# The first block's mixers: input and output projections as three one-pass products of split operands

## The chip, the cores and the metric

The kernel runs on one core of a Trainium2 chip. The core has TensorE (matrix products), VectorE, ScalarE and GpSimd (elementwise work, on their own instruction queues) and SyncE, whose queue issues the weight DMAs. The profile calls them PE (and PEld for weight loads), DVE, ACT, POOL and SP. The metric is the device time of one execution in microseconds.

## The reference

Two transformer blocks of two layers each, D = 1024, 256 tokens, all in fp32. The change is in the mixer of the first block; one of its layers, cut:

```python
h = h + 0.5 * swiglu(rmsnorm(h, ffn1_norm[i]), ...)                  # ffn1
u = rmsnorm(h, mix_norm[i]) @ w_in[i]                                # input projections
c_q, c_kv, k_rope, m_x, m_v, m_o, m_if, f_in = split_cols(u, IN_SPLITS)
y_mla = mla_mixer(c_q, c_kv, k_rope, ...)                            # attention, 4 heads
y_mlstm = mlstm_mixer(m_x, m_v, m_o, m_if, ...)                      # conv, gates, two scans
y_fnet = fnet_mixer(f_in, fnet_w[i], fnet_b[i])                      # DFT as products
h = h + jnp.concatenate([y_mla, y_mlstm, y_fnet], axis=-1) @ w_out[i]  # out projection
h = h + 0.5 * swiglu(rmsnorm(h, ffn2_norm[i]), ...)                  # ffn2
```

`w_in` is 1024 x 1744, `w_out` 1024 x 1024. Then follows a gated embedding (`ple`), and after both layers the second block.

## The kernel before

Activations lie feature-major: eight tiles of 128 features by 256 tokens. Weights come as chunks of 128 x 2048 fp32 (1 MB) in a fixed order through a ring of four slots; SyncE loads the next chunk into a slot when that slot's `used` semaphore says so. All engines run one hand-ordered program each, stage after stage (`ffn1`, `mix1`, `ffn2`, `ple` per layer), with waits on semaphores; PSUM is two groups of four banks, `low` and `high`, used in turn.

In the FFNs the products are of split operands: ScalarE copies a chunk to a rounded type that TensorE multiplies in one pass (`split_high`, line 774, into `w_split`), VectorE subtracts that from the chunk (`split_low`, line 811), the same is done with the activations (`x_split`, `a_split`), and `mm3` adds high x high, high x low and low x high. A split chunk frees its ring slot at once; two split buffers alternate, and ScalarE waits on `split_used` for TensorE. Each FFN has 33 chunks, the last 11 of them for the down product (48 one-pass products of 256 columns a chunk).

In the mixer stage `mix1` the products are plain fp32, straight from the ring. `mix1_tensor` first takes `first_projection` (chunk 0, eight k steps of two products, each k as soon as ScalarE has written `xn` for it, line 1190), then the sum of the squares, which GpSimd has added up (line 1221), then chunk 1, the gates (chunk 2, also the conv products), chunk 3 (the m_v values), chunks 4 and 5, the latent sums, chunks 6 and 7 with gate rows between. Each of these chunks but the gates' has 16 products of 128 x 128 by 256 columns. Attention, mLSTM and Fourier mixing follow, and `out_projection` (four chunks, 64 products; source `sq`). VectorE evicts and scales most of it (line 2104), ScalarE the rest; in `mix1_vector`, `head_out` (lines 2162 to 2167) makes the mLSTM output, `transposed_probs` (line 2189) copies a head's transposed softmax for TensorE's value product, and after the out projection each of eight tiles is added to h (line 2310), followed by the low part of the next FFN's x (`plain_low_parts`, line 1205); ScalarE makes the high part (line 1187) and the squares (line 1194). Both also do the next FFN's first two chunk splits between these tiles, after tiles 4 to 6.

At the end of `ffn1` VectorE adds each of the eight down tiles to h (line 1170) and ScalarE follows with `xn` and the square. In layer 0 the rotary table is made just ahead of this (`setup_vector`, lines 4628 to 4650, then `setup_scalar`, lines 4659 to 4661).

Of the kernel before, what the change touches and what calls it, by code (L numbers as in the profile page):

```python
# [25 lines left out]
P = 128  # L26
# [368 lines left out]
def split_count(kind):  # L395
# [33 lines left out]
    "ada_part",  # L429
    "square_in", "square_sum", "plain_root", "gate_part", "gate_scaled", "gate_act", "up_part", "up_scaled", "act_ready", "scale_cols", "rinv_done",  # L430
# [124 lines left out]
class Shared:  # L555


    def __init__(self, nc, ctx, args):
# [6 lines left out]
        self.ring = sb("ring", [P, SLOTS, CHUNK])  # L565
# [19 lines left out]
        with ExitStack() as halves:  # L585
# [7 lines left out]
            self.half_ring = sb_halves("half_ring", [P, 2, 2, KT, P], F32R)  # L593

# [778 lines left out]
def plain_ffn_scalar(act, l, kind):  # L1373
# [91 lines left out]
    if kind == "ffn1":  # L1465
        plain_prepare_scalar(act, g.vec(f"mix_norm{l}"), ready, split=False)
# [14 lines left out]
def plain_ffn_vector(dve, l, kind):  # L1481
# [107 lines left out]
    dve.skip("high", FT)  # L1589
    for j in range(KT):  # L1590
        side = "low" if j < 4 else "high"
        dve.wait_ge(g.sem[side + "_full"], dve.tiles[side] + 1)
        residual_add(dve, j, dve.tile(side), side, 0.5, g.first_x if kind == "ffn1" and l == 0 else None)


def mix1_buffers(g):
# [42 lines left out]

def mix1_tensor(pe, l, kind):  # L1640
# [3 lines left out]
    xn = g.xn  # L1644
# [21 lines left out]
    def feature_pair():  # L1666
        w = weights(KT, 256)
        feature_tile(w, 0)
        feature_tile(w, 1)
        pe.release()  # L1670
        return pe.tiles["low"]

# [54 lines left out]
    first_projection(pe)  # L1727
    plain_sum_tensor(pe)
    feature_pair()
# [21 lines left out]
    w = weights(KT, 256)  # L1751
    for t in range(2):
        tile = low_tile()
        for k in range(KT):
            pe.mm(tile[:, 0:256], xn[:, k, t * P:(t + 1) * P], w[:, k, :], k == 0, k == KT - 1,
                  full="low" if k == KT - 1 else None)
    pe.release()
# [10 lines left out]
    feature_pair()  # L1768
    rope_tile = feature_pair()
# [3 lines left out]
    w = weights(KT, 256)  # L1773
# [9 lines left out]
    pe.release()  # L1783
# [7 lines left out]
    w = weights(KT, 256)  # L1791
# [3 lines left out]
    pe.release()  # L1795
# [125 lines left out]
def mix1_scalar(act, l, kind):  # L1921
# [2906 lines left out]
```

## Time and profile before

| | us |
|---|---|
| median of 3 runs | 3188.19 (3186.05 to 3196.56) |
| the profiled execution | 3193.88 (span 3192.1) |
| TensorE busy | 3150.0, 99% |
| VectorE, ScalarE, GpSimd busy | 1949.2, 1276.8, 97.3 |
| mean granted TensorE clock | 0.997 |
| mix1, layer 0 | 203.0 to 353.8 |
| mix1, layer 1 | 774.8 to 925.4 |

A timeline row gives the start in us, the duration, the engine, the line, the operation with the tiles it writes and reads, its shape and how many instructions are merged in it; in brackets stands the idle time before it and who ended it. A plain fp32 product has two records, so x32 are 16 products; a one-pass product has one. Nearly all matmuls go through one helper (line 526), so tiles tell them apart.

### The profile page before, as it was taken

How to read it: one execution, taken by the hardware profiler on the slowest of the kernel's cores; microseconds unless marked ns; L12 is line 12 of the kernel's file. 1: busy time of each engine (PE TensorE's matmuls, PEld its weight loads, DVE VectorE, ACT ScalarE, POOL GpSimd, SP SyncE). 2: the span in 40 equal slices, each digit the busy share in tenths (PEclk: the TensorE clock that was granted, in tenths of full speed). 3: DMA queues.
4: the chain of work that ended last, by engine and by line, in shares of the span. 5: the costliest groups of instructions: out<-in, count | busy, mean ns of one | idle time of the engine just before them, and what ended most of it. 6: DMA issues, size and time to landing. Idle time of an engine off the chain costs nothing.

```text
span 3192.1 us, 53025 instructions
## 1 busy us (share of the span) xinstructions
PE 3150.0 (99%) x21274; PEld 2685.9 (84%) x21274; DVE 1949.2 (61%) x2974; ACT 1276.8 (40%) x1999; POOL 97.3 (3%) x106
## 2 busy tenths in 40 slices
PE   9999999999999999999999999999999999999999
PEld 8997889889778988888788888878887888876899
DVE  6755574774457556767776677557744676346444
ACT  5444454553345462222544344442224222244433
POOL 0000000000010010000000000000000000000000
PEclk9999999999999999999999999999999999999999
DMA  7543454454345435545222000035532444221353
GB/s 270 184 146 142 175 185 171 178 186 157 139 172 179 176 119 190 185 171 191 93 80 80 3 3 3 28 127 190 205 124 79 171 186 183 97 74 40 134 183 131
DMA packets 62489, 441.25 MB, mean 138 GB/s; under 512 B 6769, under 2 KB 8945, under 8 KB 9329
## 3 DMA queue, kind: packets, MB, share of 16 engines
q1 hardware_dynamic: 60992, 437.39, 37.6%
q8 instruction: 126, 2.06, 0.3%
q10 hardware_dynamic: 1328, 1.46, 0.1%
q14 instruction: 43, 0.34, 0.0%
HBM read 437.77 MB, written 1.05 MB: 137 GB/s over the span
## 4 chain that ended last, share of the span: by engine, by line
PE 91%; DVE 4%; ACT 3%; issue 1%; DMA 0%; POOL 0%; DVEq 0%; ACTq 0%; SPq 0%; POOLq 0%
PE ps_high L526 47%; PE ps_low L526 43%; PE ps_high L535 1%; ACT sb_w_split L774 1%; DVE sb_w_split L811 0%; DVE sb_arena L2151 0%; PE ps_low L535 0%; DVE sb_x_split L2908 0%; ACT sb_arena L2816 0%; DVE sb_silu L2926 0%; ACT sb_xn L2807 0%; DMA sb_ring<-weights 0%; DVE sb_arena L2114 0%; DVE sb_rinv L4495 0%; ACT sb_arena L1972 0%
## 5 line engine op out<-in xcount | busy, mean ns | idle before, releaser
L774 ACT ACTIVATE sb_w_split<-sb_ring 128x2048 fp32r<-128x2048 f32 x260 | 498.6, 1918 | 890.6 <-PE ps_low L526 697.5
L811 DVE TENSOR_TENSOR sb_w_split<-sb_ring,sb_w_split 128x2048 fp32r<-128x2048 f32 x260 | 597.6, 2298 | 257.1 <-ACT sb_w_split L774 257.1
L526 PE MATMUL ps_low<-sb_x_split,sb_w_split 128*128 128x512 f32 (+1 forms) x3520 | 691.2, 354 | 8.3 <-DVE sb_w_split L811 4.0
L526 PE MATMUL ps_high<-sb_x_split,sb_w_split 128*128 128x512 f32 (+1 forms) x3520 | 686.9, 353 | 0.3 <-DVE sb_w_split L811 0.3
L526 PEld LDWEIGHTS ps_low<-sb_x_split,sb_w_split 128*128 128x128 f32 x3520 | 579.0, 189 | 108.0 <-DVE sb_x_split L2908 6.0
L526 PEld LDWEIGHTS ps_high<-sb_x_split,sb_w_split 128*128 128x128 f32 x3520 | 580.3, 189 | 94.7 <-DVE sb_w_split L811 0.6
L526 PE MATMUL ps_low<-sb_a_split,sb_w_split 128*128 128x256 f32 (+1 forms) x2112 | 370.2, 325 | 0.0
L526 PE MATMUL ps_high<-sb_a_split,sb_w_split 128*128 128x256 f32 (+1 forms) x2112 | 365.7, 323 | 0.0
L526 PEld LDWEIGHTS ps_low<-sb_a_split,sb_w_split 128*128 128x128 f32 x2112 | 314.2, 190 | 37.6 <-DVE sb_w_split L811 2.6
L526 PEld LDWEIGHTS ps_high<-sb_a_split,sb_w_split 128*128 128x128 f32 x2112 | 314.9, 190 | 30.9
L1024 DVE SCALAR_TENSOR_TENSOR sb_rest<-sb_ring,sb_consts 128x1024 f32<-128x1024 f32 x256 | 313.3, 1224 | 27.1 <-DVE sb_rest L1024 7.7
L526 PE MATMUL ps_low<-sb_xn,sb_ring 128*128 128x256 f32 (+1 forms) x800 | 183.7, 388 | 0.5 <-ACT sb_xn L2840 0.5
L526 PEld LDWEIGHTS ps_low<-sb_xn,sb_ring 128*128 128x128 f32 x800 | 151.3, 190 | 29.9 <-issue 10.2
L526 PE MATMUL ps_high<-sb_x_split,sb_half_ring 128*128 128x512 f32 x720 | 171.5, 394 | 0.0
L1109 DVE TENSOR_TENSOR sb_a_split<-sb_arena,sb_a_split 128x1024 fp32r<-128x1024 f32 (+1 forms) x44 | 48.0, 1091 | 193.9 <-ACT sb_a_split L1057 193.9
L526 PEld LDWEIGHTS ps_high<-sb_x_split,sb_half_ring 128*128 128x128 f32 x720 | 133.0, 188 | 26.8
L1102 DVE TENSOR_TENSOR sb_arena<-sb_silu,ps_high 128x512 f32 (+3 forms) x88 | 54.5, 620 | 88.8 <-PE ps_high L526 88.8
L1532 DVE TENSOR_TENSOR sb_a_split<-sb_arena,sb_a_split 128x512 fp32r<-128x512 f32 x44 | 30.4, 691 | 111.7 <-ACT sb_a_split L1402 111.7
L1049 ACT ACTIVATE sb_silu<-ps_low 128x512 f32<-128x512 f32 (+1 forms) x88 | 46.9, 533 | 111.4 <-PE ps_low L526 111.4
L2757 POOL TENSOR_TENSOR sb_arena<-sb_arena 128x512 f32<-128x512 f32 (+1 forms) x27 | 33.7, 1250 | 1795.6 <-ACT sb_arena L2816 1793.9
L526 PE MATMUL ps_high<-sb_sq,sb_ring 128*128 128x256 f32 x384 | 83.6, 380 | 1.6 <-issue 1.6
L526 PEld LDWEIGHTS ps_high<-sb_sq,sb_ring 128*128 128x128 f32 x384 | 72.7, 190 | 12.6 <-issue 2.9
(404 smaller groups left out, 3221.0 us busy)
## 6 DMA issues: line engine op xcount, KB each, us to landing
sb_ring<-weights SPq DMA_DIRECT2D x412, 1024.0 KB, 4.8
sb_consts<-consts SPq DMA_DIRECT2D x1, 2148.0 KB, 18.3
sb_sq<-xT SPq DMA_DIRECT2D x1, 1024.0 KB, 5.6
sb_ring<-weights SPq DMA_DIRECT2D x2, 512.0 KB, 7.5
sb_h<-ctxT ACTq DMA_DIRECT2D x1, 1024.0 KB, 15.5
out<-sb_h SPq DMA_DIRECT2D x1, 512.0 KB, 3.0
sb_vectors<-vectors ACTq DMA_DIRECT2D x1, 269.0 KB, 5.8
out<-sb_h SPq DMA_DIRECT2D x1, 256.0 KB, 2.6
```

The source lines that it names most:

```text
L526: ins = self.g.nc.tensor.matmul(out, lhsT, rhs, start=start, stop=stop)
L535: ins = self.g.nc.tensor.transpose(out, in_, self.g.const("identity")[0:n, 0:n])
L774: g.nc.scalar.activation(g.w_split[:, 0, s % 2, :], g.ring[:, n % SLOTS, :], ACT.Copy).then_inc(g.sem["w_high"], 1)
L811: g.nc.vector.tensor_tensor(g.w_split[:, 1, s % 2, :], g.ring[:, n % SLOTS, :], g.w_split[:, 0, s % 2, :].bitcast(F32), ALU.subtract).then ...
L1024: ins = g.nc.vector.scalar_tensor_tensor(scratch, tiles[:, op // STREAMS, :], 1.0, rows[:, op % STREAMS, :], ALU.mult, ALU.mult, accum_out ...
L1049: nc.scalar.activation(g.silu[:, f % 2, 0:width], g.banks["low"][(low + f) % 4][:, 0:width], ACT.Silu).then_inc(g.sem["low_free"], 1)
L1102: nc.vector.tensor_tensor(out, g.silu[:, f % 2, 0:width], g.banks["high"][(high + f) % 4][:, 0:width], ALU.mult).then_inc(g.sem["high_free ...
L1109: nc.vector.tensor_tensor(g.a_split[:, 1, c % 2, :, 0:width], act_in[:, bass.ds(at, 2), 0:width], g.a_split[:, 0, c % 2, :, 0:width].bitca ...
L1532: v.tensor_tensor(g.a_split[:, 1, c % 2, :, 0:TOK], act_in[:, bass.ds(at, 2), 0:TOK], g.a_split[:, 0, c % 2, :, 0:TOK].bitcast(F32), ALU.s ...
L2757: g.nc.gpsimd.tensor_tensor(squares[:, 0, 0:width], squares[:, k, 0:width], squares[:, 0, 0:width], ALU.add).then_inc(g.sem["norm_sum"], p ...
```

## The change

The seven large input chunks (`MIXER_INPUTS`, all but the gates') and the four output chunks are split too. ScalarE writes a chunk's high part (`mixer_split_scalar`) into a half of `w_split` or into `gates_high`, a new buffer over part of the arena; VectorE writes the low part over the chunk in its ring slot (`ring_low`), so the slot is free only when TensorE is done with it, as before. TensorE does `mm3` with both. x is split by `plain_prepare_scalar(..., split=True)` and `plain_low_parts` at the end of `ffn1`; `xn` is no longer made. The gates stay in fp32 and take the high and the low part of x one after the other. The mixed outputs are split as well: ScalarE writes the high part and VectorE subtracts, for the four heads both straight from PSUM, where before ScalarE alone copied the value product into `sq`. The arena's buffers get another order. The core of the diff:

```diff
@@ plain_ffn_scalar, behind after_down @@
     if kind == "ffn1":
-        plain_prepare_scalar(act, g.vec(f"mix_norm{l}"), ready, split=False)
+        for m in (1, 0):
+            mixer_split_scalar(act, l, m, act.chunks + FFN_CHUNKS, act.splits + FFN_CHUNKS)
+        plain_prepare_scalar(act, g.vec(f"mix_norm{l}"), ready, split=True)
@@ plain_ffn_vector, behind setup_vector @@
+    if kind == "ffn1":
+        for m in (1, 0):
+            mixer_split_vector(dve, m, dve.chunks + FFN_CHUNKS, dve.splits + FFN_CHUNKS)
     for j in range(KT):
...
         residual_add(dve, j, dve.tile(side), side, 0.5, g.first_x if kind == "ffn1" and l == 0 else None)
+        if kind == "ffn1" and j:
+            plain_low_parts(dve, g.vec(f"mix_norm{l}"), j - 1, "mix1", l)
+    if kind == "ffn1":
+        plain_low_parts(dve, g.vec(f"mix_norm{l}"), KT - 1, "mix1", l)
@@ new @@
+def mixer_split_scalar(act, l, m, first, splits):
+    g = act.g
+    n = first + MIXER_CHUNKS[m]
+    act.wait_ge(g.landed[n % SLOTS], 16 * (n // SLOTS + 1))
+    if m == 0:
+        act.wait_ge(g.sem["split_used"], splits - 1)
+    elif m == 1:
+        act.wait_ge(g.used[(first - 1) % SLOTS], (first - 1) // SLOTS + 1)
+    elif m == 2:
+        act.wait_ge(g.sem["split_used"], splits)
+    else:
+        act.wait_ge(g.sem["mixer_used"], MIXER_SPLITS * l + m - 1)
+    g.nc.scalar.activation(mixer_high(g, splits, m), g.ring[:, n % SLOTS, :],
+                           ACT.Copy).then_inc(g.sem["mixer_high"], act.adds("mixer_high"))
+
+def mixer_split_vector(dve, m, first, splits):
+    g = dve.g
+    n = first + MIXER_CHUNKS[m]
+    dve.wait_ge(g.sem["mixer_high"], dve.due("mixer_high"))
+    g.nc.vector.tensor_tensor(g.ring_low[:, n % SLOTS, :], g.ring[:, n % SLOTS, :],
+                              mixer_high(g, splits, m).bitcast(F32),
+                              ALU.subtract).then_inc(g.sem["mixer_low"], dve.adds("mixer_low"))
@@ mix1_tensor: feature_tile, likewise the m_v product; first_projection becomes first_pair @@
-            pe.mm(tile[:, 0:TOK], w[:, k, m * P:(m + 1) * P], xn[:, k, 0:TOK], k == 0, k == KT - 1,
-                  full="low" if k == KT - 1 else None)
+            mm3(pe, tile[:, 0:TOK], [part[:, k, m * P:(m + 1) * P] for part in w], mixer_x(g, k), k == 0, k == KT - 1,
+                full="low" if k == KT - 1 else None)
@@ the gates @@
+            for n, x in enumerate(mixer_x(g, k, slice(t * P, (t + 1) * P))):
+                last = k == KT - 1 and n == 1
+                pe.mm(tile[:, t * GATE_SPREAD:(t + 1) * GATE_SPREAD], x.bitcast(F32),
...
@@ mix1_tensor, end @@
-    pe.wait_ge(g.sem["mix_done"], pe.due("mix_done", 2))
+    pe.wait_ge(g.sem["mixed_low"], pe.due("mixed_low", 4))
     pe.wait_ge(g.sem["low_free"], pe.tiles["low"])
-    out_projection(pe, TOK)
+    mixer_out_projection(pe)
@@ mix1_scalar: chunks 2 to 6 behind the root, the second Silu, the m_v evictions and each set of squares; then @@
     root(LH)
+    for k in (6, 7):
+        mixed_high(act, k, g.sq[:, k, 0:TOK])
+    for p in range(2):
+        act.wait_ge(g.sem["mix_done"], act.due("mix_done"))
+        mixed_high(act, 4 + p, g.sq[:, 4 + p, 0:TOK])
+        mixer_split_scalar(act, l, len(MIXER_INPUTS) + p, act.chunks, act.splits)
     ada_units_scalar(act, 0, rows, 1)
...
-        evict(g.sq[:, h, 0:TOK])
+        act.wait_ge(g.sem["low_full"], act.tiles["low"] + 1)
+        mixed_high(act, h, act.tile("low", peek=True)[:, 0:TOK])
+        act.other_frees("low")
@@ mix1_vector: 2 and 3 behind the level memset, 4 behind gate_abs, 5 ahead of latents[4], 6 behind k_rope; then @@
     head_out(1)
+    for k in (6, 7, 4):
+        mixed_low_of(k)
+    mixer_split_vector(dve, len(MIXER_INPUTS), dve.chunks, dve.splits)
+    mixed_low_of(5)
+    mixer_split_vector(dve, len(MIXER_INPUTS) + 1, dve.chunks, dve.splits)
     transposed_probs(1)
+    ada_units_vector(dve, 1)
     transposed_probs(2)
+    head_low(0)
+    ada_sum_vector(dve)
     transposed_probs(3)
-    ada_units_vector(dve, 1)
-    for h in range(H):
-        if h == 1:
-            ada_sum_vector(dve)
-        dve.skip("low")
+    for h in range(1, H):
+        head_low(h)
@@ the loop over the eight out tiles, ScalarE and VectorE alike @@
+        if j in (1, 3):
+            mixer_split_vector(dve, len(MIXER_INPUTS) + 2 + j // 2, dve.chunks, dve.splits)
```

The numbers m in the split functions count the split chunks: m = 0 and 1 are chunks 0 and 1 of the stage, m = 2 to 6 are chunks 3 to 7, m = 7 to 10 the four output chunks.

## Rows read from the trace of the kernel before

**Rows 1.** The page: busy time of each engine, and the chain by engine.
```profile
PE 3150.0 (99%) x21274; PEld 2685.9 (84%) x21274; DVE 1949.2 (61%) x2974; ACT 1276.8 (40%) x1999; POOL 97.3 (3%) x106
PE 91%; DVE 4%; ACT 3%; issue 1%; DMA 0%; POOL 0%; DVEq 0%; ACTq 0%; SPq 0%; POOLq 0%
```
**Rows 2.** Timeline of TensorE, 203 to 222 us: start, us, engine, line, operation, count.
```profile
203.04 7.07 PE L526 MATMUL ps_low<-sb_xn,sb_ring 128*128 128x256 f32 x32
...
210.37 7.07 PE L526 MATMUL ps_low<-sb_xn,sb_ring 128*128 128x256 f32 x32
217.28 0.38 PE L535 MATMUL ps_high<-sb_consts,sb_rinv 128*128 128x128 f32 x2
217.50 3.68 PE L526 MATMUL ps_low<-sb_ring,sb_xn 128*128 128x64 f32 x32
221.02 1.95 PE L526 MATMUL ps_high<-sb_arena,sb_ring 128*128 128x256 f32 x8
```
**Rows 3.** Timeline at the end of the first FFN of each layer.
```profile
201.99 0.49 ACT L1190 ACTIVATE sb_xn<-sb_h,sb_vectors 128x256 f32<-128x256 f32 x1
...
766.64 2.28 DVE L811 TENSOR_TENSOR sb_w_split<-sb_ring,sb_w_split 128x2048 fp32r<-128x2048 f32 x1
...
774.84 7.07 PE L526 MATMUL ps_low<-sb_xn,sb_ring 128*128 128x256 f32 x32
```
**Rows 4.** Timeline of TensorE, out projection and the FFN behind it, layer 0.
```profile
326.25 27.86 PE L526 MATMUL ps_high<-sb_sq,sb_ring 128*128 128x256 f32 x128 [0.52 <-issue]
353.76 5.91 PE L526 MATMUL ps_low<-sb_x_split,sb_w_split 128*128 128x512 f32 x32
359.50 5.80 PE L526 MATMUL ps_high<-sb_x_split,sb_w_split 128*128 128x512 f32 x32
```
**Rows 5.** Timeline of TensorE in a down product, layer 0.
```profile
137.91 1.59 PE L526 MATMUL ps_low<-sb_a_split,sb_w_split 128*128 128x256 f32 x12
...
143.66 1.60 PE L526 MATMUL ps_low<-sb_a_split,sb_w_split 128*128 128x256 f32 x12
```
**Rows 6.** Timeline at the end of attention, layer 0.
```profile
319.67 0.42 DVE L2167 TENSOR_TENSOR sb_sq<-sb_sq,sb_arena 128x256 f32<-128x256 f32 x1
320.01 1.28 DVE L2189 COPY sb_arena<-ps_high 128x512 f32<-128x512 f32 x2
320.75 1.13 PE L526 MATMUL ps_low<-sb_arena 128*128 128x256 f32 x4 [2.55 <-DVE sb_arena L2189]
```
**Rows 7.** Groups by line: the two halves of a weight chunk's split.
```profile
L774 ACT ACTIVATE sb_w_split<-sb_ring 128x2048 fp32r<-128x2048 f32 x260 | 498.6, 1918 | 890.6 <-PE ps_low L526 697.5
L811 DVE TENSOR_TENSOR sb_w_split<-sb_ring,sb_w_split 128x2048 fp32r<-128x2048 f32 x260 | 597.6, 2298 | 257.1 <-ACT sb_w_split L774 257.1
```
**Rows 8.** Timeline beside the out projection: VectorE, GpSimd and ScalarE.
```profile
345.14 0.73 POOL L1221 TENSOR_TENSOR sb_root<-sb_rest,sb_root 128x256 f32<-128x256 f32 x1 [2.73 <-ACT sb_rest L1194]
...
347.98 2.28 DVE L811 TENSOR_TENSOR sb_w_split<-sb_ring,sb_w_split 128x2048 fp32r<-128x2048 f32 x1
348.59 2.25 POOL L1221 TENSOR_TENSOR sb_root<-sb_rest,sb_root 128x256 f32<-128x256 f32 x1 [2.73 <-ACT sb_rest L1194]
...
350.69 0.42 DVE L2310 TENSOR_TENSOR sb_h<-ps_high,sb_h 128x256 f32<-128x256 f32 x1 [0.43 <-PE ps_high L526]
351.04 0.47 DVE L1205 SCALAR_TENSOR_TENSOR sb_x_split<-sb_h,sb_vectors,sb_x_split 128x256 fp32r<-128x256 f32 x1
351.15 0.51 ACT L1187 ACTIVATE sb_x_split<-sb_h,sb_vectors 128x256 fp32r<-128x256 f32 x1 [2.64 <-DVE sb_h L2310]
```
**Rows 9.** Timeline in the middle of the projections, layer 0.
```profile
241.14 0.42 DVE L2104 TENSOR_TENSOR sb_arena<-ps_low,sb_rinv 128x256 f32<-128x256 f32 x1
...
244.40 2.32 PE L526 MATMUL ps_high<-sb_sq,sb_consts 128*128 128x256 f32 x10
```
**Rows 10.** Busy time by stretch; the third number from the end is the granted clock.
```profile
322.00:323.00 1.00, 1.00 (x5) 0.91 (x4) 0.43 (x1) 0.30 (x1) 0.00 (x0) 0.50 0.30 123
...
324.00:325.00 1.00, 1.00 (x4) 0.79 (x3) 0.00 (x0) 0.38 (x1) 0.00 (x0) 0.50 0.00 0
```

More of the change, by code:

```diff
@@ new lines, in mixer_split_vector, with mixer_weights @@
+def mixer_split_vector(dve, m, first, splits):
[5 more added lines that the diff above has]
+                              ALU.subtract).then_inc(g.sem["mixer_low"], dve.adds("mixer_low"))
+def mixer_weights(pe, m):
+    g = pe.g
+    pe.wait_ge(g.sem["mixer_low"], pe.due("mixer_low"))
+    low = g.ring_low[:, pe.chunks % SLOTS, :]
+    pe.chunks += 1
+    return [part.rearrange("p (k n) -> p k n", k=KT) for part in (mixer_high(g, pe.splits, m), low)]
@@ new lines, in mixer_release, with mixer_x, mixed_parts, mixed_high @@
+def mixer_release(pe):
+    pe.release()
+    pe.unreleased.append(pe.g.sem["mixer_used"])
+def mixer_x(g, k, cols=slice(0, TOK)):
+    return [g.x_split[:, 0, k, half][:, cols] for half in (RIGHT, LEFT)]
+def mixed_parts(g, k):
+    return [g.x_split[:, 1, k, half] for half in (RIGHT, LEFT)]
+def mixed_high(act, k, source):
+    g = act.g
+    g.nc.scalar.activation(mixed_parts(g, k)[0], source, ACT.Copy).then_inc(g.sem["mixed_high"], act.adds("mixed_high"))
+def mixed_low(dve, k, source):
+    g = dve.g
+    dve.wait_ge(g.sem["mixed_high"], dve.due("mixed_high"))
+    high, low = mixed_parts(g, k)
+    return g.nc.vector.tensor_tensor(low, source, high.bitcast(F32), ALU.subtract)
@@ new lines, in mixer_out_projection @@
+def mixer_out_projection(pe):
+    g = pe.g
+    for c in range(KT // 2):
+        w = mixer_weights(pe, len(MIXER_INPUTS) + c)
+        for m in range(2):
+            pe.wait_ge(g.sem["high_free"], pe.tiles["high"] - 3)
+            tile = pe.open("high")
+            for k in range(KT):
+                mm3(pe, tile[:, 0:TOK], [part[:, k, m * P:(m + 1) * P] for part in w], mixed_parts(g, k), k == 0, k == KT - 1,
+                    full="high" if k == KT - 1 else None)
+        mixer_release(pe)
@@ L1643, in mix1_tensor @@
     rotate = g.const("rotate")
-    xn = g.xn
     rows = ada_rows_mix1(g)
@@ L1754, in mix1_tensor @@
         for k in range(KT):
-            pe.mm(tile[:, 0:256], xn[:, k, t * P:(t + 1) * P], w[:, k, :], k == 0, k == KT - 1,
-                  full="low" if k == KT - 1 else None)
-    pe.release()
+            mm3(pe, tile[:, 0:256], mixer_x(g, k, slice(t * P, (t + 1) * P)), [part[:, k, :] for part in w], k == 0, k == KT - 1,
+                full="low" if k == KT - 1 else None)
+    mixer_release(pe)
     pe.wait_ge(g.sem["low_free"], gate_tile)
@@ L1794, in mix1_tensor @@
     feature_tile(w, 1)
-    pe.release()
+    mixer_release(pe)
     decay_rows(2)
@@ L1979, in mix1_scalar @@
     plain_root_scalar(act)
+    mixer_split_scalar(act, l, 2, act.chunks, act.splits)
     act.skip("low", 4)
@@ L2012, in mix1_scalar @@
         square(b["latents"][:, k, :], g.sq[:, k, 0:TOK])
+    mixer_split_scalar(act, l, 5, act.chunks, act.splits)
     act.skip("low", 2)
@@ L2016, in mix1_scalar @@
         square(b["latents"][:, k, :], g.sq[:, k, 0:TOK])
+    mixer_split_scalar(act, l, 6, act.chunks, act.splits)
     root(Q_LORA)
@@ L2210, in mix1_vector @@
     step(v.memset(b["level"][0:H], 1.0))
+    mixer_split_vector(dve, 2, dve.chunks, dve.splits)
+    mixer_split_vector(dve, 3, dve.chunks, dve.splits)
     dve.skip("low", 3)
@@ L2225, in mix1_vector @@
     step(v.scalar_tensor_tensor(b["gate_t"][0:H], b["gate_f"][0:H], -1.0, b["gate_f"][0:H], ALU.mult, ALU.max), "gate_abs")
+    mixer_split_vector(dve, 4, dve.chunks, dve.splits)
     projected(b["latents"][:, 2, :])
```

89 lines of the change are left out of this document (63 added, 26 removed).

## The prediction

> **What bounds the kernel now.** I read the busy shares and the chain of work that ended last first [rows 1]: TensorE is busy 99% of the span and carries 91% of the chain, so time goes away only where TensorE has less to do, and any new wait of TensorE is paid in full. Then the timeline, to see what TensorE does in the first block's mixer stage, which the change rewrites. There are two such stages, one per layer, 203 to 354 us and 775 to 925 us; the second repeats the first with starts 571.8 us later [rows 2, 3]. Four things are to be seen there.
>
> First, products of plain fp32 operands. Sixteen of them (x32 in the row: each has two records) run from 210.37 to 217.28 us [rows 2], 6.91 / 16 = 0.432 us each; the out projection, 64 of them from 326.25 until the next FFN's first product at 353.76 [rows 4], gives 0.430. Second, the same shape as one-pass products of split operands stands in the FFN's down product: 48 from 137.91 to 143.66 us [rows 5], 5.75 / 48 = 0.120 us each. Third, at both ends of the stage TensorE hands over with no gap: the last down product is followed at 203.04 by the first projection [rows 2], though ScalarE, held by the rotary setup, gets to the first normed tile only at 201.99 [rows 3]. Fourth, at the end of attention TensorE waits for VectorE: last gating product at 319.67, copy of the transposed probabilities at 320.01, and only then the next value product at 320.75, behind an idle of 2.55 us [rows 6]. Work added to VectorE's queue right there is on the path.
>
> **The change, part by part.** All prices are per layer unless said.
>
> *Products.* Seven input chunks and four output chunks have 16 products each, 176. Each becomes three of 0.120, 0.360 us for 0.432: 176 x 0.072 = 12.7 us less. The gate product keeps fp32 and reads both halves of x: 16 products become 32. They took 217.50 to 221.02 = 3.52 us [rows 2], so +3.5. Net of TensorE's own work: -9.15 us, -18.3 for both layers.
>
> The row gives 0.120 us for a pass. The Trainium skill (FP8 and Floating Point Precision, TensorE Precision Notes) says that true fp32 takes four passes through the array; three passes for four would make 0.324 us of 0.432, and 352 products would save 12.7 us more than by the row. By that rule the sum below would end at about -0.7 us, and the row, a quarter above a bare ratio of passes, speaks against it.
>
> *Splits.* Each of the 11 chunks now costs a ScalarE copy of 1.92 us and a VectorE subtraction of 2.30 us [rows 7], put into queues that had none here. 25 us of VectorE time per stage is affordable in sum (VectorE is busy 61% [rows 1]); what counts is where the queue is in front of something TensorE needs.
>
> *Join 1, FFN to projection, layer 1.* After its last down split VectorE is free at 766.64 + 2.28 = 768.92 [rows 3]. The high part of chunk 1 waits for just that: ScalarE 768.97 to 770.9, then chunk 0 to 772.7; VectorE's low parts 770.95 to 773.2 and to 775.4. Only behind them, in program order, stands the residual add that started early before. First add 0.42, high part of x 0.51, low part 0.47 [rows 8], hand-overs 0.1: TensorE starts at 776.9 where it started at 774.84: 2.1 us. *Layer 0* has the rotary setup in front: ScalarE leaves it at 202.0 [rows 3], splits until 205.8, VectorE until 208.4, first x at 209.9 for 203.04: 6.9 us, 4.8 more than in layer 1.
>
> *Pace of the first projection.* Add and low part start 0.35 us apart and the pair takes about 0.80 us [rows 8]; TensorE needs six products, 0.72. That alone ends the chunk 0.5 us later than its products. But the sum of squares runs on GpSimd (0.73 us each) at the same time, and the rows show what happens when they meet: GpSimd's addition takes 2.25 instead of 0.73 us while VectorE's 2.28 us subtraction of two SBUF operands runs [rows 8]. Seven additions against six low parts, fully in turn: 6 x (0.47 + 0.73 + 0.1 - 0.80) = 3.0 more, 3.6 us. Starts overlap somewhat, so I take 1.65, bounds 0.5 and 3.6. The Trainium skill (SBUF — State Buffer, Who interferes with whom) says the same of such a pair: one fully blocks. By it alone the term would be its upper bound, 3.6, and 3.9 us would be added to the sum for both layers; the row agrees on the blocking and leaves open how much of it shows.
>
> *Middle.* Feature pairs keep TensorE 1.15 us shorter each. The splits of chunks 2, 3, 4 and 6 fall into waits of VectorE. That of chunk 5 stands in front of the fourth latent tile: before, VectorE had it at 241.14 and the latent sums came at 244.40 with 2.8 us to spare [rows 9]; now TensorE reaches them relatively earlier and VectorE 2.3 later. A stall of 0.8 us, bounds 0 and 1.5. The ring of four slots is not late: three chunks of 5.76 us each lie between the release of a slot and its next use.
>
> *Join 2, attention.* Behind the last gating product VectorE now has four low parts (0.42 each, starts 0.35 apart) and two chunk splits before it may copy the transposed probabilities: 4 x 0.35 + 2 x 2.25 = 5.9 us, so the copy starts at 325.9 instead of 320.01. From there to the out projection it was 6.24 us (320.01 to 326.25 [rows 4, 6]); ScalarE's and VectorE's reads of the same PSUM bank add one VectorE step, 0.45. Sum 6.35; copies that slide together give back some: I take 6.0. In those 6.24 us TensorE ran at half its clock: the granted clock was 0.50 from 322 on and still at 324, behind the 2.5 us idle [rows 10], 1.2 instead of 2.4 GHz. At full clock the tail would be 5.2, so 4.85 is the lower bound; if the half clock, behind an idle that is now 8 us, covers all head products and transposes too, 7.7.
>
> *Out projection and next FFN.* 64 products are 4.6 us shorter (in the net above). The splits of the third and fourth chunk stand between the adds: from the start of the stage, tile 1 at 5.8, its add 6.4, ScalarE's high part 7.2 to 9.1, low part to 11.4, TensorE needs it at 11.5: no wait. The fourth: add of tile 3 at 12.6, high part 13.4 to 15.3, low part to 17.7, needed at 17.3: 0.4. Then the next FFN's first two splits follow, which had 3.45 us between tiles and now 2.88: low part of x tile 6 at 29.4, needed at 27.7: 1.75. Sum 2.2, bounds 1.0 and 3.5. Before, nothing was late there: the FFN's first chunk ran from 353.76 to 359.50, 5.74 us [rows 4].
>
> *Sum.* Per layer -9.15 + 2.1 + 1.65 + 0.8 + 6.0 + 2.2 = +3.6. Two layers +7.2, layer 0's setup +4.8: **+12.0 us**. Lower ends: -9.15 + 2.1 + 0.5 + 0 + 4.85 + 1.0 = -0.7, so +3.4; upper ends: +9.25, so +23.3. Against the profiled execution (3193.9) that is 3205.9; against the median of the runs, which is 5.7 lower, 3200.2. A measurement tells about 0.3%, 9.6 us, from no change.
>
> **Rivals.**
> 1. *The joins are cheap.* GpSimd and VectorE slip past each other, the heads run at full clock: the lower ends, +0 to +7, some 3193. For it: those terms are bounds, none is a row of this very pattern.
> 2. *The joins are dear.* Half clock through the heads and the first projection chunk, VectorE and GpSimd in strict turn: +17 to +25, some 3210. For it: the clock fell behind only 2.5 us of idle.
> 3. *Faster: the queues are ahead at the joins.* Place: VectorE's queue at 768.9 and at 320.1. If it has its splits done before TensorE finishes its own work there, joins 1 and 2 and the tail cost nothing and the net of the products is left: -18.3, 3170. It decides from 2.1 us of earlier VectorE work at join 1 (6.9 in layer 0) and 5.9 at join 2; the first is fixed by the wait for the last down split, the second by the order of the queue, so the profile speaks against it.
> 4. *The products take three quarters.* 0.324 us: -12.7, near 3187.5, no change. Against it 48 products in 5.75 us. The Trainium skill's TensorE Precision Notes, cited above, lead here.
> That the products are not one pass after all would show as two records each; the w_split rows, of the same type, have one [rows 5].
>
> **How the numbers follow.** The forecast, +7 to +17, has 0.55; rival 1 0.21; rival 2 0.12; rival 3 0.08; rival 4 0.04. The predicted time is the forecast's, 3200.2. Range 3187 to 3213: it takes in rivals 1 and 4, the upper end up to +25, and leaves rival 3 and some outliers. Slower by over 9.6 us: three quarters of the forecast and rival 2, 0.53. Faster: rival 3 and a little of others, 0.10. The rest, 0.37, within 0.3%.
>
> **What would show it.** Right: after the first FFN TensorE idle 6 to 7 us in layer 0 and about 2 in layer 1, put down to VectorE; a feature pair at 5.76 us; the gates at 7.0; the idle before the second head's value product 8 us instead of 2.5, and the start of the out projection about 6 us later against the last gating product; 64 products in 23 to 25 us; an idle of 1 to 2 us in the next FFN's first chunk. Wrong: a pair at 5.2 us (rival 4), no idle at the joins (rival 3), or a granted clock at half for long stretches of the projections (rival 2). I am least sure of the clock and of VectorE against GpSimd.

## The result, and the profile after

The changed kernel takes 3210.3 us (median of 4 runs, 3206.8 to 3211.4) against 3190.0 of the kernel before beside it (4 runs, 3186.1 to 3196.6). The ratio is 1.0064, 95% interval 1.0049 to 1.0078: 20.3 us slower. The two profiled executions, 3206.8 and 3193.9 us, are 12.9 apart. The forecast was 12.0 by that second measure, and 3200.2 us in medians, which is 10.1 short of the measured median but with it inside the range.

The page's busy time and the chain by engine, after:
```profile
PE 3137.4 (98%) x21690; PEld 2689.8 (84%) x21690; DVE 2010.5 (63%) x3028; ACT 1320.0 (41%) x2029; POOL 97.5 (3%) x106
PE 87%; DVE 6%; ACT 4%; issue 1%; POOL 0%; DMA 0%; DVEq 0%; ACTq 0%; SPq 0%; POOLq 0%
```
TensorE is busy 12.6 us less than in [rows 1] and the span is 12.9 longer: work went, waiting came. The waits of TensorE say who is blamed (us in total, times, longest):
```profile
PE ps_low L527 <- DVE sb_x_split L1212: 11.3, 4, 6.8
PE ps_low L527 <- ACT sb_xn L2839: 9.0, 2, 4.5
PE ps_low L527 <- DVE sb_arena L2327: 6.7, 2, 3.3
PE ps_high L527 <- ACT sb_sq L2083: 2.2, 2, 1.1
```
Timeline of TensorE, layer 0; these starts answer to [rows 2, 4, 6, 9]:
```profile
209.76 0.55 PE L527 MATMUL ps_low<-sb_x_split,sb_w_split 128*128 128x256 f32 x1 [6.77 <-DVE sb_x_split L1212]
...
217.66 0.59 PE L527 MATMUL ps_high<-sb_root,sb_consts 128*128 128x256 f32 x2
217.91 0.47 PE L527 MATMUL ps_low<-sb_x_split,sb_gates_high 128*128 128x256 f32 x1
...
223.75 0.38 PE L536 MATMUL ps_high<-sb_consts,sb_rinv 128*128 128x128 f32 x2
...
231.06 0.43 PE L527 MATMUL ps_high<-sb_arena,sb_ring 128*128 128x256 f32 x1
...
253.27 1.10 PE L527 MATMUL ps_high<-sb_sq,sb_consts 128*128 128x256 f32 x4 [1.12 <-ACT sb_sq L2083]
...
324.51 0.60 PE L536 MATMUL ps_high<-sb_consts,sb_arena 128*128 128x128 f32 x4
329.59 0.60 PE L527 MATMUL ps_low<-sb_consts,sb_xn 128*128 128x8 f32 x2 [4.48 <-ACT sb_xn L2839]
333.53 2.07 PE L527 MATMUL ps_low<-sb_arena 128*128 128x256 f32 x4 [3.34 <-DVE sb_arena L2327]
...
339.80 0.48 PE L527 MATMUL ps_high<-sb_x_split,sb_w_split 128*128 128x256 f32 x2 [1.05 <-issue]
...
363.00 4.32 PE L527 MATMUL ps_low<-sb_x_split,sb_w_split 128*128 128x512 f32 x24
368.60 1.68 PE L527 MATMUL ps_low<-sb_x_split,sb_w_split 128*128 128x512 f32 x8 [1.28 <-DVE sb_x_split L1212]
370.12 1.09 PE L527 MATMUL ps_high<-sb_x_split,sb_w_split 128*128 128x512 f32 x5
```
The bracket is the idle before the row. The two joins (6.77; 4.48 and 3.34 us), the latent sums (1.12) and the next FFN's first chunk (1.28) are where TensorE stands. In layer 1 the first join is shorter and the others repeat:
```profile
787.79 0.56 PE L527 MATMUL ps_low<-sb_x_split,sb_w_split 128*128 128x256 f32 x2 [2.01 <-DVE sb_x_split L1212]
...
916.04 0.47 PE L527 MATMUL ps_high<-sb_x_split,sb_w_split 128*128 128x256 f32 x2 [1.05 <-issue]
```
Busy time by stretch, after; the third number from the end is the granted clock:
```profile
205.00:210.00 5.00, 0.24 (x1) 0.27 (x2) 4.75 (x7) 1.90 (x5) 0.00 (x0) 0.78 0.00 0
210.00:215.00 5.00, 5.00 (x26) 5.00 (x27) 4.97 (x12) 4.71 (x13) 4.03 (x6) 0.54 0.01 3
...
270.00:275.00 5.00, 5.00 (x14) 3.08 (x13) 2.74 (x6) 2.44 (x9) 0.00 (x0) 0.76 0.24 39
325.00:330.00 5.00, 0.52 (x3) 0.41 (x2) 4.89 (x8) 4.14 (x5) 0.00 (x0) 0.72 0.85 360
330.00:335.00 5.00, 1.66 (x5) 1.30 (x6) 4.40 (x6) 0.18 (x1) 0.00 (x0) 0.50 0.00 0
335.00:340.00 5.00, 3.95 (x16) 3.06 (x15) 1.87 (x4) 1.15 (x3) 0.00 (x0) 0.75 0.01 2
```
From 210 to 215 us TensorE is busy all the time, at 0.54. From 325 to 340 the clock averages 0.66; before, it was at half from 322 to some 325.4 us [rows 10]. From 272 to 276 it stood at 0.50 with TensorE busy throughout.

The ledger, from starts of equal rows in both timelines (us, layer 0 / layer 1):

| stage | before | after | difference |
|---|---|---|---|
| idle at the first join | 0 | 6.77 / 2.01 | +6.8 / +2.0 |
| first projection | 6.9 | 7.90 / 7.26 | +1.0 / +0.35 |
| chunks 1, 3 to 7 (six) | 41.5 per layer, six of 6.9 | six of 5.7 | -7.2 / -7.2 |
| gates | 3.7 | 7.3 | +3.6 / +3.6 |
| latent sums | 2.15 | 3.3 | +1.2 / +1.2 |
| rest of attention | 52.7 | 54.4 / 52.7 | +1.7 / 0 |
| third transpose to out projection | 8.8 / 8.6 | 15.3 / 15.9 | +6.5 / +7.3 |
| out projection | 27.5 | 23.2 | -4.3 / -4.3 |
| next FFN's first chunk | 5.7 / 5.9 | 7.1 | +1.4 / +1.3 |
| sum | | | +10.7 / +4.2 |

That is 14.9 us at the end of the two stages. Behind them, between two equal rows at 1159.59 and 1170.71 us of the kernel before, the changed kernel's profiled execution wins 3.1 back (and loses about 1 near the end of the second block, which wasn't traced further). The kernel before had a stretch of lowered clock there, with TensorE busy throughout, which the changed one's profiled execution has not. It had a second one around 1535 us, which the changed one shares (0.58 and 0.74 in its two stretches from 1545 to 1555):
```profile
1160.00:1165.00 5.00, 5.00 (x23) 4.58 (x23) 2.52 (x4) 3.64 (x9) 0.00 (x0) 0.66 0.86 331
...
1535.00:1540.00 5.00, 5.00 (x19) 4.55 (x19) 0.18 (x1) 1.85 (x5) 0.00 (x0) 0.50 0.02 3
```
A trace of the kernel before with ten filler products added (run 11) has neither stretch, so they come and go from one execution to the next and aren't put down to the change.

Added up over stretches of 5 us, (1 - clock) times the length says where the clock went. Kernel before: 3.4 us at the two attention joins, 3.4 from 1160 to 1170, 3.4 from 1530 to 1545. Changed kernel: 3.4 and 1.7 behind the first joins, 5.2 and 5.1 at the attention joins, 1.7 from 270 to 280, 3.4 from 1545 to 1555. Part of both sums lies under idle time, where it costs nothing.

### The profile page after: what moved, and what is told of

Read it like the earlier page. It is cut to its first block, busy times and chain, and to the rows that moved or that the text cites. A ratio compares the mean times of both kernels' runs of the same rounds, so it can differ in the third digit from the quotient of the medians.

```text
span 3205.0 us, 53971 instructions
## 1 busy us (share of the span) xinstructions
PE 3137.4 (98%) x21690; PEld 2689.8 (84%) x21690; DVE 2010.5 (63%) x3028; ACT 1320.0 (41%) x2029; POOL 97.5 (3%) x106
## 4 chain that ended last, share of the span: by engine, by line
PE 87%; DVE 6%; ACT 4%; issue 1%; POOL 0%; DMA 0%; DVEq 0%; ACTq 0%; SPq 0%; POOLq 0%
PE ps_high L527 45%; PE ps_low L527 42%; DVE sb_w_split L818 1%; DVE sb_ring_low L1694 1%; ACT sb_w_split L781 1%; PE ps_high L536 0%; DVE sb_arena L2289 0%; PE ps_low L536 0%; DVE sb_x_split L3067 0%; DVE sb_silu L3085 0%; POOL sb_arena L2916 0%; ACT sb_w_split L1685 0%; ACT sb_gates_high L1685 0%; DVE sb_arena L2252 0%; DMA sb_ring<-weights 0%
## 5 line engine op out<-in xcount | busy, mean ns | idle before, releaser
L527 PE MATMUL ps_low<-sb_x_split,sb_w_split 128*128 128x512 f32 (+1 forms) x3840 | 753.6, 349 | 18.6 <-DVE sb_x_split L1212 11.3
L527 PEld LDWEIGHTS ps_low<-sb_x_split,sb_w_split 128*128 128x128 f32 x3840 | 631.0, 190 | 120.1 <-issue 12.9
L527 PE MATMUL ps_high<-sb_x_split,sb_w_split 128*128 128x512 f32 (+1 forms) x3648 | 710.1, 351 | 2.4 <-issue 2.1
L527 PEld LDWEIGHTS ps_high<-sb_x_split,sb_w_split 128*128 128x128 f32 x3648 | 599.9, 189 | 97.6 <-issue 2.8
L527 PE MATMUL ps_low<-sb_xn,sb_ring 128*128 128x256 f32 (+1 forms) x416 | 98.2, 396 | 0.5 <-ACT sb_xn L2999 0.5
L527 PEld LDWEIGHTS ps_low<-sb_xn,sb_ring 128*128 128x128 f32 x416 | 79.0, 190 | 19.7 <-issue 9.5
L4100 DVE SCALAR_TENSOR_TENSOR sb_arena<-sb_arena,sb_vectors 128x512 f32<-128x512 f32 x96 | 72.2, 752 | 3.4
L1390 ACT ACTIVATE sb_silu<-ps_low 128x256 f32<-128x256 f32 x88 | 32.6, 381 | 101.0 <-PE ps_low L527 100.6
```

Source lines behind the costliest of these rows:

```text
L527: ins = self.g.nc.tensor.matmul(out, lhsT, rhs, start=start, stop=stop)
L1390: nc.scalar.activation(g.silu[:, f % 2, TOK:2 * TOK], g.banks["low"][(low + f) % 4][:, rest], ACT.Copy).then_inc(g.sem["gate_part"], 1)
L4100: ins = v.scalar_tensor_tensor(out, x[:, :, k:k + TOK], taps[:, tap + k:tap + k + 1], out, ALU.mult, ALU.add)
```

## The experiments

Each gives the median of its runs beside runs of the kernel before (3188.3 to 3189.4); "less" is against the changed kernel's 3210.3 unless said. Beside that one the kernel before took 3190.0, so a difference to 3210.3 is uncertain by 1 to 2 us.

**1. ScalarE's eviction, or VectorE's queue?** The wait table blames ScalarE for 4.48 us per layer.
```diff
+    ada_units_scalar(act, 0, rows, 1)
     for k in (6, 7):
         mixed_high(act, k, g.sq[:, k, 0:TOK])
...
-    ada_units_scalar(act, 0, rows, 1)
```


> Whole computation. Of the changed kernel only one thing is moved: ScalarE's eviction of the conditioning rows (L2839), which stood behind two chunk copies, goes ahead of them. The wait table puts 9.0 us of TensorE's idle at the attention join (4.48 in each layer) down to it. Theory A, VectorE's queue is last anyway: the copy of the transposed probabilities still starts at 332.8 behind four low parts and two chunk subtractions, so the two idles of 4.48 and 3.34 us become one of about 7.8 and the out projection starts where it did: span within 2 us of 3205. Theory B, ScalarE's queue is the cause, as the wait table says: 4.5 us come back in each layer, 9 in all, about 3196.

3208.7 us (one run), span 3206.0. TensorE's row behind the join:
```profile
331.14 2.07 PE L527 MATMUL ps_low<-sb_arena 128*128 128x256 f32 x4 [8.29 <-DVE sb_arena L2327]
```
The two idles became one of 8.29 us. ScalarE's eviction was late behind two chunk copies, but with it out of the way TensorE waits as long; VectorE's queue decides. In the changed kernel it reads:
```profile
327.04 1.09 DVE L1735 TENSOR_TENSOR sb_x_split<-sb_sq,sb_x_split 128x256 fp32r<-128x256 f32 x3
328.05 2.29 DVE L1694 TENSOR_TENSOR sb_ring_low<-sb_ring,sb_w_split 128x2048 fp32r<-128x2048 f32 x1
329.28 0.26 ACT L2839 ACTIVATE sb_xn<-ps_low 128x128 f32<-128x128 f32 x1
330.25 0.42 DVE L1735 TENSOR_TENSOR sb_x_split<-sb_sq,sb_x_split 128x256 fp32r<-128x256 f32 x1
330.58 2.29 DVE L1694 TENSOR_TENSOR sb_ring_low<-sb_ring,sb_gates_high 128x2048 fp32r<-128x2048 f32 x1
332.79 1.28 DVE L2327 COPY sb_arena<-ps_high 128x512 f32<-128x512 f32 x2
```
Four low parts and two chunk subtractions, 5.75 us, and only then the copy at 332.79.

**2. The attention join alone repaired.** Run 1's move of ScalarE's eviction is part of it.
```diff
@@ mix1_scalar, behind the second absolute()
+    act.wait_ge(g.sem["high_full"], act.tiles["high"])
+    mixer_split_scalar(act, l, len(MIXER_INPUTS), act.chunks, act.splits)
@@ mix1_vector
     read = [peak(0), peak(1)]
+    mixer_split_vector(dve, len(MIXER_INPUTS), dve.chunks, dve.splits)
...
+    transposed_probs(1)
+    ada_units_vector(dve, 1)
+    transposed_probs(2)
     for k in (6, 7, 4, 5):
         mixed_low_of(k)
...
     for h in range(1, H):
         head_low(h)
+    mixer_split_vector(dve, len(MIXER_INPUTS) + 1, dve.chunks, dve.splits)
```


> Whole computation. The changed kernel with the attention join alone repaired: the first output chunk is split in gaps that both engines have during attention (ScalarE idle 302.9 to 309, VectorE idle 309.7 to 314.6), VectorE copies the transposed probabilities before its low parts, and the second output chunk is split behind the heads. Theory: the queue was the whole of it. From the third transpose to the out projection 15.3 us (15.9 in layer 1) go back to 9.2, a little more than the 8.8 of before, and with the idle goes the half clock behind it: 12.5 us less than the changed kernel, range 10 to 15. Rival: the half clock comes from elsewhere, or the early split only moves the wait forward into the head norm: less than 8 us back.

3195.6 us (10 runs, 3193.3 to 3200.4; ratio to the kernel before 1.0022, 1.0012 to 1.0031): 14.7 less. VectorE's early subtraction, and TensorE at the join:
```profile
307.72 2.29 DVE L1694 TENSOR_TENSOR sb_ring_low<-sb_ring,sb_w_split 128x2048 fp32r<-128x2048 f32 x1
...
325.91 1.66 PE L527 MATMUL ps_low<-sb_arena 128*128 128x256 f32 x4 [2.54 <-DVE sb_arena L2329]
...
331.93 0.47 PE L527 MATMUL ps_high<-sb_x_split,sb_w_split 128*128 128x256 f32 x2 [1.05 <-issue]
```
The subtraction sits in what was an idle of 4.94 us; TensorE's idle is 2.54, that of [rows 6]. From the third transpose to the out projection 9.3 and 8.3 us.

**3. The first join alone repaired.**
```diff
-        act.wait_ge(g.used[(first - 1) % SLOTS], (first - 1) // SLOTS + 1)
+        act.wait_ge(g.used[(first - 3) % SLOTS], (first - 3) // SLOTS + 1)
@@ plain_ffn_vector, plain_ffn_scalar
-    if kind == "ffn1" and l == 0:
-        setup_vector(dve)          # and setup_scalar(act)
@@ mix1_vector, start; mix1_scalar, behind the split of chunk 3
+    if l == 0:
+        setup_vector(dve)          # and setup_scalar(act)
```


> Whole computation. The changed kernel with the first join alone repaired: the split of the first two input chunks no longer waits for the FFN's last down split (its buffer is free two chunks earlier), and the rotary setup of layer 0 stands behind the first projection's low parts. Theory: idle 6.77 us (layer 0) and 2.01 us (layer 1) go to under 0.5 each, the granted clock stays 1.00 behind them, and the first projection takes 6.7 us in both layers (7.90 and 7.26 before), the rest over 5.7 being VectorE against GpSimd: 10.5 us less than the changed kernel, range 8.5 to 12.5. Rival: the first chunk's pace is all clock, none of it GpSimd: 5.8 us for it, 12.5 less. Rival: the setup moved behind delays the reciprocal and takes 1 to 2 us back.

3199.2 us (9 runs, 3197.3 to 3200.5; 1.0029, 1.0018 to 1.0039): 11.1 less.
```profile
203.96 0.47 PE L527 MATMUL ps_low<-sb_x_split,sb_w_split 128*128 128x256 f32 x2 [0.26 <-DVE sb_x_split L1212]
...
210.75 0.60 PE L527 MATMUL ps_high<-sb_root,sb_consts 128*128 128x256 f32 x2
```
Idle 0.26 us, first projection 6.79 at full clock in layer 0 and 6.77 in layer 1. So of the changed kernel's 7.90 and 7.26 us, 1.1 and 0.5 were clock.

**4. The clock alone, at the attention join.**
```diff
         if h == 1:
+            stream_ahead(pe, "low", 17)
             ada_sum_tensor(pe, 0, rows)
```


> Whole computation, with 17 products of constants added per layer, written to a bank that is overwritten. The changed kernel, with TensorE kept busy (17 plain fp32 products of 0.432 us, 7.3 us) in the 7.8 us in which it waits at the attention join; no queue is changed. It prices the clock alone. Theory: granted clock 1.00 from 325 on instead of 0.50 from 327 to 337.5; the four products and transposes behind the wait, 6.3 us in layer 0 and 6.9 in layer 1, take 4.5 to 5: 4 us less than the changed kernel, range 3 to 6. Rival: the clock costs nothing here, since these steps wait for VectorE's and ScalarE's copies: 0 to 1 us less.

3203.5 us (4 runs, 3201.3 to 3206.1): 6.8 less, above the range of 3 to 6.
```profile
333.46 1.13 PE L527 MATMUL ps_low<-sb_arena 128*128 128x256 f32 x4 [0.96 <-DVE sb_arena L2328]
...
337.99 0.47 PE L527 MATMUL ps_high<-sb_x_split,sb_w_split 128*128 128x256 f32 x2 [1.05 <-issue]
...
330.00:335.00 5.00, 4.04 (x23) 3.52 (x22) 4.33 (x6) 0.55 (x2) 0.00 (x0) 1.00 0.00 0
```
Granted clock 1.00. From the third transpose to the out projection 13.55 us in both layers for 15.3 and 15.9: the half clock behind the wait costs 4.1 us in both layers together. The kernel before pays 2.9 of the same kind (run 11), so of the 13.8 us that this join lost, 1.2 are clock and the rest is wait. The trace places only 4.1 of the 6.8 us at the join; the rest stays open.

**5. The kernel before with the join's burden.**
```diff
     head_out(1)
+    for _ in range(2):
+        settle()
+        spare = g.consts[:, 0:CHUNK]
+        step(v.tensor_tensor(g.w_split[:, 1, 0, :], spare, spare, ALU.subtract))
     transposed_probs(1)
```


> The kernel before, whole, plus two VectorE subtractions of 128x2048 per layer (a scratch result, 2.3 us each) put in front of the copy of the transposed probabilities: the attention join's burden alone, with none of the products split. Theory: VectorE's queue is the price whatever TensorE multiplies with. The idle of 2.55 us becomes 7.1, the half clock behind it grows from 3.4 to 6.8 or 10.2 us: 4.6 and 0.5 to 1.7 us in each layer, 11 us more than the kernel before, range 10 to 13. Rival: TensorE's products behind the join have slack against something else, so that under 6 us show.

3200.8 us (5 runs, 3199.2 to 3201.5) against 3188.4: 12.3 more.
```profile
325.27 2.08 PE L526 MATMUL ps_low<-sb_arena 128*128 128x256 f32 x4 [7.19 <-DVE sb_arena L2189]
...
331.80 1.53 PE L526 MATMUL ps_high<-sb_sq,sb_ring 128*128 128x256 f32 x6 [0.52 <-issue]
```
The idle is 7.19 us for the 2.55 of [rows 6]. From the third transpose to the out projection it is 14.5 and 14.1 us for 8.8 and 8.6, 11.1 more in both layers. Most of the 13.8 us that the join lost arises with no product split and 4.6 us of VectorE work for 5.75, so it belongs to the order of the queue.

**6. Four repairs together.**
```diff
@@ beside edits 2 and 3: mix1_vector
-    mixer_split_vector(dve, 5, dve.chunks, dve.splits)
     projected(b["latents"][:, 4, :])
     projected(b["k_rope"])
+    mixer_split_vector(dve, 5, dve.chunks, dve.splits)
...
-        if j in (5, 6):
+        if j == 5:
...
     plain_low_parts(dve, g.vec(f"ffn2_norm{l}"), KT - 1, "ffn2", l)
+    split_low(dve, 1)
```


> Whole computation. Both joins repaired as in the two runs before, and two smaller waits: the low part of input chunk 5 goes behind the two projected tiles that the latent sums wait for (1.12 us of idle in each layer), and the next FFN's second split goes behind its last x tile (1.28 us). Theory: the terms add. 14.7 and 11.1 us from the two joins, as measured, and 2 x 2.4: 30.6 less than the changed kernel, about 3180, 8 to 9 less than the kernel before. Rival: half clock or the waits come back elsewhere, or the moved low part makes chunk 5 late: no more than 26 less, no difference from the kernel before.

ScalarE's half of the next FFN's second split moves too, from tile 6 to tile 7.

3180.9 us (10 runs, 3179.0 to 3182.7); to the kernel before 0.9977 (0.9968 to 0.9986), faster by 7.6 us. The terms add: 29.4 of 30.6. TensorE's idle in front of the chunk behind the latent sums:
```profile
246.18 0.51 PE L527 MATMUL ps_low<-sb_x_split,sb_w_split 128*128 128x256 f32 x2 [0.56 <-DVE sb_ring_low L1690]
```
Half of the latent sums' 1.12 us stays, as the moved low part is now what comes last; the next FFN's idle is gone.

**7. GpSimd against VectorE.**
```diff
-                    plain_sum_pool(pool)
+                    plain_sum_pool(pool, 8 if kind == "mix1" else TOK)
```


> The four repairs, with GpSimd's seven additions in front of the mixer cut to 8 of 256 columns, so the sum of squares for the first block's mixer norm is left out in most columns. It asks what sets the pace of the first projection, 6.78 us for 5.7 at full clock in both layers. Theory, GpSimd holds VectorE up: low parts take 0.48 instead of 0.62 to 0.67 us and the projection 5.9: 0.9 less in each layer, 1.8 us in all. Rival, VectorE's own chain of an add and a low part (0.80 us for TensorE's 0.71) is the limit: 6.4, 0.4 less in each layer.

3179.5 us (7 runs, 3176.4 to 3181.7), 1.4 less than with four repairs, a difference smaller than either kernel's spread; the reading rests on the traces. GpSimd's additions and a low part of x there, then the same low part here:
```profile
204.88 5.13 POOL L1228 TENSOR_TENSOR sb_root<-sb_rest,sb_root 128x256 f32<-128x256 f32 x6
205.27 0.63 DVE L1212 SCALAR_TENSOR_TENSOR sb_x_split<-sb_h,sb_vectors,sb_x_split 128x256 fp32r<-128x256 f32 x1
```
```profile
205.11 0.47 DVE L1212 SCALAR_TENSOR_TENSOR sb_x_split<-sb_h,sb_vectors,sb_x_split 128x256 fp32r<-128x256 f32 x1
```
The first projection takes 5.80 us for 6.78. GpSimd's sum costs 1.0 us per layer, nearly all of the pace's excess over its products (5.7).

**8. The gates as one-pass products.**
```diff
-                pe.mm(tile[:, t * GATE_SPREAD:(t + 1) * GATE_SPREAD], x.bitcast(F32),
-                      w[:, k * 16:k * 16 + GATE_SPREAD], ...)
+            mm3(pe, tile[:, t * GATE_SPREAD:(t + 1) * GATE_SPREAD], mixer_x(g, k, slice(t * P, (t + 1) * P)),
+                [part[:, k * 16:k * 16 + GATE_SPREAD] for part in gate_parts(g)], ...)
```


> Whole computation. As the run with four repairs, and the gate product too is made of three one-pass products of split operands: 48 of 64 columns for 32 plain ones that took 7.1 us. What a one-pass product of 64 columns takes no row shows. By columns it would be 0.03 us, bounded below by what loads the next operand; the plain one of 64 columns takes 0.22. Taking 0.06 to 0.12 us, 2.9 to 5.8 us for 7.1: 1.3 to 4.2 us less in each layer, 3 taken, so 6 less than the run with four repairs. Rival: operand loads set the pace at 0.117 us as for 256 columns: 3 less.

3182.8 us (11 runs, 3180.0 to 3188.0), 2.0 more than with four repairs; the two kernels' runs overlap, so what is shown is that the 6 us didn't come.
```profile
216.74 5.83 PE L527 MATMUL ps_low<-sb_x_split 128*128 128x64 f32 x48
222.37 3.37 PE L527 MATMUL ps_high<-sb_arena,sb_ring 128*128 128x256 f32 x8
...
222.00:225.00 3.00, 3.00 (x9) 2.54 (x9) 2.96 (x5) 2.88 (x6) 0.00 (x0) 0.50 0.03 8
```
48 products in 5.63 us, 0.117 each: 64 columns cost what 256 do (192 in 23.2 us in the out projection, 0.121). The 1.5 us gained here is lost at once. In the stretch from 222 to 225 TensorE is busy all 3 us at a granted clock of 0.50, and the convolution's products take 3.0 us for 1.6. In layer 1 the clock falls amid the gates, at 788.7 us: the 48 products take 7.27 us (785.14 to 792.41), no less than the 32 plain ones they replace, and the convolution's again 3.0. Other runs of this kernel lie at a mean clock of 0.994 to 0.996, those with four repairs at 0.997 to 0.998.

**9. Half of the gate products.**
```diff
-            for n, x in enumerate(mixer_x(g, k, slice(t * P, (t + 1) * P))):
+            for n, x in enumerate(mixer_x(g, k, slice(t * P, (t + 1) * P))[:1]):
```


> The four repairs, with the gate product reading only the high half of x, 16 plain products for 32 in each layer: the low half's share of the gates is left out. Theory: nothing stands beside them, so each of the 32 products left out gives its 0.22 us: 3.5 us a layer, 7 less than the kernel with four repairs, about 3174. Rival: the value projection's split or the convolution's result is late behind shorter gates, and part of it becomes a wait: 3 to 5 less.

3177.2 us (4 runs, 3176.4 to 3178.7), 3.7 less than with four repairs where 7 were expected.
```profile
216.81 3.68 PE L527 MATMUL ps_low<-sb_ring,sb_x_split 128*128 128x64 f32 x32
222.00 2.97 PE L527 MATMUL ps_high<-sb_arena,sb_ring 128*128 128x256 f32 x8 [1.50 <-ACT sb_arena L2106]
```
TensorE is done with the gates at 220.5 and waits 1.50 us for ScalarE's activation of the convolution, and then runs below full clock (0.50 from 223 to 226). In layer 0, where VectorE has the moved setup ahead of the convolution, the gates' full length covers that wait; in layer 1 the convolution isn't late, and the value projection's split only by 0.19 us.

**10 and 11. The clock at the remaining wait**, with five products of constants ahead of it: `stream_ahead(pe, "low", 5)` in the place of run 4's 17, in the kernel with four repairs and in the kernel before.

> Whole computation, with five products of constants added per layer, written to a bank that is overwritten. The kernel with four repairs, and TensorE kept busy (2.2 us) in the wait of 2.55 us that the attention join has in every kernel here. Theory: the half clock of 3.4 us behind it goes in both layers and with it 1 us each: 2 less than the kernel with four repairs, about 3179, range 3177 to 3180. Rival: since the steps behind that wait hang on copies, nothing: 3181.

3180.5 us (8 runs, 3177.6 to 3187.0): no difference. At the join the filler works in the trace: 8.3 us from the third transpose to the out projection in both layers, for 9.3 and 9.2 in run 6. But TensorE stands at 0.50 for some 3.5 us in three places behind products over 4 rows (from 255, 821 and 832 us), where run 6's trace has none.

> The kernel before, whole, with the same five products of constants in the same wait. Theory: 1 us less in each layer, 2 in all, as the half clock from 322 to 325.4 us goes. Rival: nothing. It also says whether the best version owes its lead to this alone.

3188.9 us (11 runs, 3185.0 to 3192.1); to the kernel before 0.9994 (0.9985 to 1.0003): none that can be told.
```profile
325.07 1.10 PE L526 MATMUL ps_high<-sb_sq,sb_ring 128*128 128x256 f32 x4 [0.52 <-issue]
```
In the trace the filler works: from the third transpose to the out projection 7.3 us for 8.8 and 8.6. The medians don't show 2.9 us. The runs' mean clock goes with the spread: runs of this kernel at 1.000 took 3185.0 to 3186.2, those at 0.998 3189.6 to 3192.1. The runs of the kernel before at 0.999, its highest, took 3186.0 to 3188.5; the best runs of the two kernels differ by some 2 us, as expected. Lowered clock appears in other places from run to run, and why stays open.

## Why the prediction was right, and where it fell short

**Products.** Right. 64 triples took 23.2 us, from 339.80 to 363.00, 0.363 each with a wait of 0.3 among them, for the 0.360 forecast. Six chunks gave 1.2 us each, the out projection 4.3. Rival 4's 0.324 is excluded. (The prediction puts the row "a quarter above a bare ratio of passes"; 0.120 is a ninth above a quarter of 0.432. No term rests on it.)

**Gates.** 3.6 for 3.5 us. That nothing stands beside them was only nearly right: taken away again, they gave 3.7 of 7 us (run 9).

**Join 1.** 6.77 and 2.01 us for 6.9 and 2.1. Run 3 shows that the cause was as named: the wait for the last down split, and the setup.

**Pace.** 1.65 was forecast; the chunk ended 2.2 and 1.5 us later than its products. The term is 1.1 at full clock (6.79 us less 5.7), of which GpSimd is 1.0 (run 7), and the clock behind the idle, 1.1 and 0.5 us, wasn't in it. The two engines slow each other rather than take strict turns: a low part of 0.47 us takes 0.62 to 0.68, an addition of 0.73 some 0.86. The Trainium skill (SBUF — State Buffer, Who interferes with whom) calls the port pair that these two engines share an exclusive lock, which would give the upper bound of 3.6; the trace does not bear this out for operations of 256 columns.

**Middle.** 1.2 us of stall for 0.8, in its bounds; the cause was as named, and the squares of the late latent tiles were what TensorE met first.

**Join 2.** 6.5 and 7.3 us for 6.0, in its bounds, and by the queue as told (runs 1, 2 and 5). Of the 1.8 us that both layers lost beyond the forecast, 1.2 are clock (runs 4 and 11): the sum gave both kernels the same stretch of half clock, and the longer wait is followed by a longer one. (In the kernel before that stretch was 3.4 of the 6.24 us, not all of them as the prediction has it [rows 10].)

**Out projection and next FFN.** The waits are 0.3 and 1.3 us for 0.4 and 1.75.

**Rest of attention.** The sum has nothing here, and layer 0 lost 1.7 us. TensorE stood at 0.50 from 272 to 276 us, busy throughout, behind a group of products over 4 rows.

**That 12.0 met 12.9 is partly luck.** At the end of the two stages the loss was 14.9 us, 2.9 more than the sum: 1.8 at join 2, 1.7 in the rest of attention, 0.8 in the middle and 0.4 in the pace, less some 1.8 that the products and the waits of the out projection and the next FFN gave back. Then 3.1 us came back, because the profiled execution of the kernel before had one stretch of lowered clock more, and about 1 was lost at the end.

**Where it fell short is the last step of the sum**, "against the median of the runs, which is 5.7 lower". The profiled execution of the kernel before had a mean clock of 0.997, and that kernel's runs at 0.997 take 3192.0 to 3194.7 while most have 0.998 or 0.999, the latter 3186.0 to 3188.5. Its two extra stretches, at 3.1 us by the one that could be measured, are about these 5.7 us; that the faster runs lacked them is inferred from their clock, as they have no trace. The changed kernel's profiled execution was its fastest, at 0.994; the others have 0.992 and 0.993 and took 3210.1 to 3211.4. So the distance doesn't carry over: 5.7 were taken off that the new kernel doesn't give, its median is 3.5 above its profiled run, and with the 0.9 missing in the sum that makes the 10.1 us. In medians, rival 2's price of 3210 came true, but not by its mechanism: strict turns didn't come (pace), and half clock behind the joins is 1.6 us at the first and 1.2 at the second. That its number fits is luck.

**The other rivals.** Rival 1 fell with the 6.8 us of idle at join 1 and the 6.5 us lost at join 2. Rival 3 named the right lever: with the queues ahead at both joins (run 6) the split is worth having, though at 3180.9 and not 3170: the pace (1.1 us a layer), remainders of waits, and a mean clock of 0.997 to 0.998 for 0.999 stay, the last worth an estimated 3 to 6 us (0.001 to 0.002 of the span).

## What to carry to other kernels

Split products pay by TensorE's own ledger only if the splits stand in gaps of the elementwise queues: here 352 products were worth 25 us, and where the 22 splits, the low parts and the rotary setup were queued decided between 20 us slower and 8 us faster. When a wait table names an engine, ask what stands second; moving ScalarE's eviction gave nothing. Compare a profiled run with its kernel's other runs by mean clock before a difference is carried from one to the other, and compare two traces by the places where their clock is low before two spans are subtracted.

## What was not expected of the hardware

The granted clock fell to 0.50 with TensorE busy without a gap: in run 8 behind 48 one-pass products of 64 columns in layer 0 (3.00 us busy of 3.00) and among them in layer 1, and in the changed kernel from 270 to 275 us (0.76, busy 5.00 of 5.00) behind products over 4 rows. Each mixer has two groups of such products, of 512 columns. In the traces of the three kernels whose mixers multiply plain fp32 (the kernel before, runs 5 and 11) none of the 12 groups is followed by a lowered clock. In the ten traces with split products 15 of 40 are, in eight of the traces: the clock falls within 0.7 us of the group's end and stays at 0.50 for about 3.5 us. Runs 6 and 9 have none. It looks like a price of the split products that comes and goes; no run here isolates it. The page of the Trainium skill on the clock (TensorE: Matmul & The Clock Gate, HAM oscillation) speaks of idle gaps; these stretches stood in busy time. A one-pass product took 0.117 us with 64 columns as with 256, where each comes with a new stationary operand, while a plain one fell from 0.43 to 0.22.
